# A stage boundary: the scan's first operands loaded from inside the projection stage

## The chip, the cores and the metric

The kernel runs on one core of a Trainium2 chip. The time is device microseconds (us) of one execution, and the figure for a kernel is the median of several runs.

## The reference, cut to what matters

The reference is a two-layer decoder trunk for 1024 tokens of width 1024, in float32: layer 0 is attention and a mixture of experts, layer 1 is a Mamba-2 mixer and a mixture of experts. The change lies in the Mamba-2 mixer:

```python
z, xbc, dt = jnp.split(h @ w_in, [D_INNER, D_INNER + XBC_DIM], axis=-1)
xbc = jax.nn.silu(causal_depthwise_conv(xbc, conv_w, conv_b))
xs, bm, cm = jnp.split(xbc, [D_INNER, D_INNER + SSD_GROUPS * D_STATE], axis=-1)
dt = jax.nn.softplus(dt + dt_bias)
a = -jnp.exp(a_log)
y = ssd_chunked_scan(xs, dt, a, bm, cm) + d_skip[:, None] * xs
y = y.reshape(Bsz, S, D_INNER) * jax.nn.silu(z)
y = rmsnorm(y.reshape(Bsz, S, SSD_GROUPS, -1), gate_norm.reshape(SSD_GROUPS, -1))
return y.reshape(Bsz, S, D_INNER) @ w_out
```

Per chunk of the scan, with `cs` the running sum of `dt * a`: `y = (C B^T * exp(cs_i - cs_j)) (dt x) + (C state) * exp(cs)`, and the state is decayed and receives `B^T (to_end * dt x)`.

## The kernel before, in words

The layer is three stages, each in a `Stage` of its own. A stage ends with its block: every engine is done, its semaphores are cleared, and all engines meet at a barrier before the next stage's first instruction.

**Projection** (`ssd_project_stage`). TensorE works off 80 units of 24 matmuls: 48 channel units (24 tiles of 128 channels, two halves of the tokens each) and 32 gate units (4 groups of 8 token tiles). In the last group the 8 gate units come last. ScalarE evicts each unit (`evict`): a channel unit into `u`, a gate unit through SiLU into one of two buffers `z`. A channel tile is then convolved on VectorE into `acc`, and `silu` on ScalarE writes `c`. SP stores `z` to the array Z (L1202) and `c` to XC (L1206) in DRAM; the eviction of gate unit m waits until the store of gate unit m-2 has landed, since there are two `z` buffers. TensorE writes a ring of four banks, so a unit waits for the eviction of the unit four before. The running sums are stored to CSR early in the stage. Weights come through three buffers `raw`.

**Scan** (`scan_stage`). 32 items, 8 chunks of 128 tokens for each of 4 groups of 8 heads. An item is spread over four engines. ScalarE: `falls` (L1686, eight activations, one for each head, that subtract sums from sums), a copy `bt` (L1695), one exponential over all heads (L1701), and the sum of squares of an earlier item; VectorE: five or six operations, of which `W` (L1735) needs the exponential; TensorE: `front` (L1625 to L1633) and `back` (L1642 to L1657); GpSimd: the fading of the state and the gate with `z` (L1789). Inputs are loaded for four items at a time into two sets of buffers: `bT`, `cT` (256 KB each), `xT` (1 MB), and `sums` (2 MB, rows of CSR spread over all partitions). The first `sums` go in four pieces of 512 KB, whose rows are 128 numbers long, not 512. SP issues the loads in this order:

```python
operands(0)
for n in range(RING):
    gates(n)
operands(1)
early_dma(sp)
for n in range(RING, NI):
    if n % LOAD == 0 and n >= 2 * LOAD:
        operands(n // LOAD)
    gates(n)
```

`operands(q)` loads the inputs of items 4q to 4q+3, `gates(n)` the gate values `z` of item n (L1599, four buffers; from item 4 on it waits for the gate of item n-4), and `early_dma` issues half of the output weights (`w_out`, 4 MB). The sums of set q = 2 and later are issued by ScalarE (L1700) in item 4q-5.

**Output** (`ssd_out_stage`): normalization, transposes and the product with `w_out`. Then comes the mixture of experts.

Of the kernel before, what the change touches and what calls it, by code (L numbers as in the profile page):

```python
# [23 lines left out]
P = 128  # L24
D = 1024
S = 1024
NT = S // P
ND = D // P
HALF = 512
# [14 lines left out]
DI, HS, G, N, HD = 2048, 32, 4, 128, 64  # L44
HG = HS // G
XBC = DI + 2 * G * N
SSD_IN = DI + XBC + HS
CONV = 4
# [1022 lines left out]
def ssd_project_stage(nc, K, A):  # L1071
# [4 lines left out]
    LEFT, GW, CPG = CONV - 1, DI // G, DI // G // P  # L1076
    TILES = [n for g in range(G) for n in (DI // P + g, DI // P + G + g, *range(CPG * g, CPG * (g + 1)))]
    PER = CPG + 2
    NTILES, RAW, PAR, BANKS, RING = len(TILES), 3, range(2), 4, 3
    UNITS = []  # L1080
    for g in range(G):
        tiles, gates = [(False, i, h) for i in range(PER * g, PER * (g + 1)) for h in range(2)], [(True, g, t) for t in range(NT)]
        UNITS += tiles + gates if g else gates + tiles
    NU = len(UNITS)
# [3 lines left out]
    PIECES = [('gate', 0, q) for q in range(QZ)] + [('tile', 0, 0), ('dt', 0, 0), ('tile', 1, 0)]  # L1088
# [12 lines left out]
    PIECES, WHEN = [PIECES[n] for n in order], [WHEN[n] for n in order]  # L1101
    number = {p: n for n, p in enumerate(PIECES)}
    splits = {u: [n for n in range(len(PIECES)) if WHEN[n] == u] for u in range(-1, NU)}
    with Stage(nc, "sproj") as st:
        raw = [st.sb(f"raw{j}", [P, D]) for j in range(RAW)]
        with ExitStack() as early:
            hn = [early.enter_context(nc.sbuf_tensor(f"sproj_hn{a}", [P, D], F32))[:, :] for a in PAR]

# [2 lines left out]
        gh, gl = ([st.sb(f"{n}{q}", [P, 2, GW], F32R) for q in range(QZ)] for n in ("gate_high", "gate_low"))  # L1111
        dh, dl = (st.sb(n, [P, ND, HS], F32R) for n in ("dt_high", "dt_low"))
        tap = st.sb("tap", [P, NTILES, CONV + 1])
        u, acc, c = ([st.sb(f"{n}{a}", [P, w]) for a in PAR] for n, w in (("u", LEFT + S), ("acc", S), ("c", S)))
        z = [st.sb(f"z{a}", [P, GW]) for a in PAR]

        pos = st.sb("pos", [P, NT, HS])
# [15 lines left out]
        c_stored, z_stored = ([st.sem(f"{n}_stored{a}") for a in PAR] for n in "cz")  # L1133
# [40 lines left out]
        @block.sync  # L1174
        def _(sp):
            def load(n):
                if n >= RAW:
                    sp.wait_ge(w_low, n - RAW + 1)
                sp.dma_start(raw_of(n), piece(n)[0]).then_inc(raw_loaded[n % RAW], 16)

            for t in range(NT):
                for k in PAR:
                    if t >= RING:
                        sp.wait_ge(added[k], t - RING + 1)
                    r = k * S + t * P
                    sp.dma_start(rows[k][t % RING], K.Y[r:r + P, :]).then_inc(got[k][t % RING], 16)
                load(t)
            sp.dma_start(tap[:, :, :], A["conv"].rearrange("k p n -> p k n")).then_inc(tap_loaded, 16)
            load(NT)
            for v in range(0, NU + 2):  # L1190
                for n in splits.get(v, ()):
                    if n + RAW < len(PIECES):
                        load(n + RAW)
                if v == NT + 11:
                    sp.wait_ge(sums_kept, 2)
                    for h in range(2):
                        sp.dma_start(K.CSR[:, half(h)], z[h][0:HS, :]).then_inc(sums_stored, 16)
                if v >= 1 and v <= NU and UNITS[v - 1][0]:
                    _, g, t = UNITS[v - 1]
                    m = gates_before(v - 1)  # L1200
                    sp.wait_ge(evicted, v)
                    sp.dma_start(K.Z[tile(t), g * GW:(g + 1) * GW], z[m % 2][:, :]).then_inc(z_stored[m % 2], 16)  # L1202
                if v >= 2 and not UNITS[v - 2][0] and UNITS[v - 2][2] == 1:
                    i = UNITS[v - 2][1]
                    sp.wait_ge(c_ok, i + 1)
                    sp.dma_start(K.XC[TILES[i], :, :], c[i % 2][:, :]).then_inc(c_stored[i % 2], 16)  # L1206
            for a in PAR:
                sp.wait_ge(z_stored[a], 16 * (G * NT // 2))
                sp.wait_ge(c_stored[a], 16 * (NTILES // 2))
            sp.nop()  # L1210

        @block.tensor
# [293 lines left out]
def scan_stage(nc, K, A, early_dma):  # L1506


    GW, KT = HG * HD, HG * HD // P
    ITEMS = [(g, c) for g in range(G) for c in range(NT)]  # L1510
    NI, RING, LOAD = len(ITEMS), 4, 4
    with Stage(nc, "scan") as st:
        PAR = range(2)
        xT = [st.sb(f"xT{a}", [P, KT, LOAD * P]) for a in PAR]
        bT, cT = ([st.sb(f"{n}{a}", [P, LOAD * P]) for a in PAR] for n in ("bT", "cT"))
        z, y = ([st.sb(f"{n}{a}", [P, GW]) for a in range(RING)] for n in "zy")
        sums = [st.sb(f"sums{a}", [P, HG, LOAD * P]) for a in PAR]
        cbm = [st.sb(f"cbm{a}", [P, P]) for a in PAR]
        dec, W = ([st.sb(f"{n}{a}", [P, HG, P]) for a in PAR] for n in ("dec", "W"))
        bt = [st.sb(f"bt{a}", [P, N]) for a in PAR]  # L1520
# [3 lines left out]
        pcb, pbt, pyi, pst = (st.ps(n, [P, HALF]) for n in ("pcb", "pbt", "pyi", "pst"))  # L1524
        px, py = ([st.ps(f"{n}{a}", [P, GW]) for a in PAR] for n in ("px", "py"))
        z_loaded, y_stored = ([st.sem(f"{n}{a}") for a in range(RING)] for n in ("z_loaded", "y_stored"))
        loaded, sums_loaded = ([st.sem(f"{n}{a}") for a in PAR] for n in ("loaded", "sums_loaded"))
        first_sums = [st.sem(f"first_sums{j}") for j in range(LOAD)]
        cb_done, x_turned, yi_done, st_done, y_done = (st.sem(n) for n in ("cb_done", "x_turned", "yi_done", "st_done", "y_done"))
        bt_ok, e_ok, ss_ok = (st.sem(n) for n in ("bt_ready", "decay_ready", "squares"))  # L1530
        cbm_ok, seg_ok, xdt_ok, yi_ok, y_ok, st_ok = (st.sem(n) for n in ("cbm_ready", "seg_ready", "xdt_ready", "yi_ready", "y_ready", "state_ready"))
# [28 lines left out]

        def sums_here(eng, n):

            if n < LOAD:
                eng.wait_ge(first_sums[n], 16)
            else:
                q = n // LOAD
                eng.wait_ge(sums_loaded[q % 2], (q // 2 + q % 2) * 16)

        def arrived(eng, n):
            eng.wait_ge(loaded[n // LOAD % 2], (n // (2 * LOAD) + 1) * 48)  # L1570
# [1 line left out]
        @block.sync  # L1572
        def _(sp):
            def inputs(g, tok, a):
                for buf, first in ((bT, DI // P), (cT, DI // P + G)):
                    sp.dma_start(buf[a][:, :], K.XC[g + first, :, tok]).then_inc(loaded[a], 16)
                sp.dma_start(xT[a][:, :, :], K.XC[g * KT:(g + 1) * KT, :, tok].rearrange("k p n -> p k n")).then_inc(loaded[a], 16)

            def operands(q):
                (g, c), a = ITEMS[q * LOAD], q % 2  # L1580
                tok = slice(c * P, (c + LOAD) * P)
                if q >= 2:
                    sp.wait_ge(y_done, (q - 1) * LOAD)
                if q == 0:
                    for j in range(LOAD):
                        sp.dma_start(sums[0][:, :, j * P:(j + 1) * P],
                                     K.CSR[0:HG, j * P:(j + 1) * P].partition_broadcast(P)).then_inc(first_sums[j], 16)
                        if j == 0:
                            inputs(g, tok, a)
                    return  # L1590
                inputs(g, tok, a)
                if q == 1:
                    sp.dma_start(sums[a][:, :, :], spread_sums(q)).then_inc(sums_loaded[a], 16)

            def gates(n):
                (g, c), a = ITEMS[n], n % RING
                if n >= RING:
                    sp.wait_ge(gated, n - RING + 1)
                sp.dma_start(z[a][:, :], K.Z[c * P:(c + 1) * P, g * GW:(g + 1) * GW]).then_inc(z_loaded[a], 16)  # L1599

            operands(0)
            for n in range(RING):
                gates(n)
            operands(1)
            early_dma(sp)
            for n in range(RING, NI):
                if n % LOAD == 0 and n >= 2 * LOAD:
                    operands(n // LOAD)
                gates(n)

            for t in range(2):
                for g in range(G // 2):
                    m = g * NT + t
                    sp.wait_ge(y_stored[m % RING], (m // RING + 1) * 16)
                sp.dma_start(K.y_first[t][:, :, :].rearrange("p g n -> p (g n)"),
                             K.YS[t * P:(t + 1) * P, 0:DI // 2]).then_inc(K.y_loaded[t], 16)
# [186 lines left out]
def ssd_out_stage(nc, K, A):  # L1803
# [5 lines left out]
    with Stage(nc, "sout") as st:  # L1809
        w, loaded = K.w_out, K.wo_loaded  # L1810
        wh, wl = (st.sb(n, [P, NK, D], F32R) for n in ("w_high", "w_low"))
        y, y_loaded, EARLY = K.y_first, K.y_loaded, 3
        whole = [st.sb(f"whole{a}", [P, NK, P]) for a in range(2)]
        yh, yl = ([st.sb(f"{n}{a}", [P, NK, P], F32R) for a in range(2)] for n in ("y_high", "y_low"))
        tp = [st.ps(f"tp{a}", [P, NK, P]) for a in range(2)]
        py = [st.ps(f"py{a}", [P, D]) for a in range(2)]
# [132 lines left out]
def ssd_layer(nc, K, A):  # L1949
    with Stage(nc, "ssd_layer") as outer:  # L1950
        ctx, K.wo_loaded = outer.ctx, outer.sem("wo_loaded")

        def sb(name, shape):
            return ctx.enter_context(nc.sbuf_tensor(name, shape, F32))

        K.heads, K.ss = sb("heads", [P, 7, NT, HS]), sb("gate_ss", [P, NT, G])
        with ExitStack() as early:
            K.HH, K.HL = (early.enter_context(nc.sbuf_tensor(f"ssd_{n}", [P, ND, S], F32R)) for n in ("high", "low"))
            ssd_project_stage(nc, K, A)
        K.w_out = sb("w_out", [P, DI // P // 2, D])  # L1960

        K.y_first = [sb(f"y_first{a}", [P, G // 2, DI // G]) for a in range(2)]
        K.y_loaded = [outer.sem(f"y_loaded{a}") for a in range(2)]

        def out_weights(sp):
            sp.dma_start(K.w_out[:, :, :], A["w_out_ssd"][0:DI // 2, :].rearrange("(k p) n -> p k n", p=P)).then_inc(K.wo_loaded, 16)

        scan_stage(nc, K, A, out_weights)
        ssd_out_stage(nc, K, A)
# [877 lines left out]
```

## Time and profile before

| | |
|---|---|
| median of 3 runs | 2892.21 us (2891.63 to 2892.35) |
| profiled execution, its own time | 2890.16 us |
| its span | 2888.4 us |
| TensorE / VectorE / ScalarE / GpSimd busy | 92% / 65% / 56% / 19% of the span |
| mean granted TensorE clock | 0.959 |

The profile is one execution. Its own time is 1.8 us more than its span, and 2.05 us below the median of the runs. Times in the rows are microseconds from the span's start; busy shares are averages over very different stages, and the change touches only the stretch from about 1760 to 1980 us: projection until 1782, scan until about 1983.

### The profile page before, as it was taken

The numbers are of one execution on the slowest core, as the hardware profiler recorded it, in microseconds if no ns is written. First come the engines' busy times: TensorE is split into PE (matmuls) and PEld (weight loads), VectorE is DVE, ScalarE is ACT, GpSimd is POOL, SyncE is SP. The second block draws the span as 40 slices with busy tenths as digits, with TensorE's granted clock in tenths as the row PEclk, the third lists the DMA queues.
The fourth block names the chain that finished last, engine by engine and source line by source line (L and its number), as shares of the span: only waits on it lengthen the run. The fifth ranks groups of instructions, "written<-read, shape, count | busy, mean of one in ns | idle before, by whom it ended". The sixth has DMA issues, their size and how long they took to land. (4 is left out here: it accounts for less than half of the span.)

```text
span 2888.4 us, 40193 instructions
## 1 busy us (share of the span) xinstructions
PE 2652.6 (92%) x13762; PEld 2134.6 (74%) x13762; DVE 1883.1 (65%) x2208; ACT 1604.7 (56%) x2027; POOL 542.9 (19%) x462
## 2 busy tenths in 40 slices
PE   8997999987999999967999997898998799999992
PEld 6885677765888888846788885686885688888881
DVE  6335766426888888854572450686454788888895
ACT  4134554324888888854331231784122688888882
POOL 0000000001444444420000000342000344444440
PEclk9998999998999999988999998998999899999996
DMA  4315110125999999963232322984114799999994
GB/s 159 87 46 167 38 45 23 37 106 193 372 380 382 384 388 383 377 248 99 72 119 78 109 84 89 328 282 140 46 35 155 262 391 386 373 380 379 381 373 191
DMA packets 240965, 618.68 MB, mean 214 GB/s; under 512 B 31864, under 2 KB 80528, under 8 KB 240720
## 3 DMA queue, kind: packets, MB, share of 16 engines
q1 hardware_dynamic: 209712, 558.35, 53.6%
q0 software_dynamic: 19136, 33.61, 3.1%
q10 hardware_dynamic: 12000, 25.17, 2.4%
q8 instruction: 73, 1.20, 0.2%
q14 instruction: 44, 0.36, 0.0%
HBM read 566.55 MB, written 86.13 MB: 226 GB/s over the span
## 5 line engine op out<-in xcount | busy, mean ns | idle before, releaser
L2527 DVE TENSOR_TENSOR moe_w_low<-moes_raw,moe_w_high 128x2048 fp32r<-128x2048 f32 x384 | 865.0, 2286 | 147.7 <-ACT moe_w_high L2456 147.5
L2456 ACT ACTIVATE moe_w_high<-moes_raw 128x2048 fp32r<-128x2048 f32 x384 | 721.6, 1914 | 68.9 <-PEq L150 54.6
L2321 POOL COPY moe_pick<-moes_tokens 128x1 int32 (+1 forms) x64 | 108.4, 1694 | 582.9 <-PE moe_px L2370 582.0
L174 PE MATMUL moe_py<-moe_w_high,moe_h_high 128*128 128x512 f32 x512 | 209.2, 409 | 0.0
L174 PE MATMUL moe_pg<-moe_w_high,moe_x_high 128*128 128x512 f32 x512 | 205.6, 402 | 3.8 <-DVE moe_x_low L2577 3.8
L174 PE MATMUL moe_pu<-moe_w_high,moe_x_high 128*128 128x512 f32 x512 | 204.2, 399 | 0.0
L176 PE MATMUL moe_pg<-moe_w_high,moe_x_low 128*128 128x512 f32 x512 | 201.7, 394 | 0.0
L175 PE MATMUL moe_pg<-moe_w_low,moe_x_high 128*128 128x512 f32 x512 | 201.0, 393 | 0.0
L176 PE MATMUL moe_py<-moe_w_high,moe_h_low 128*128 128x512 f32 x512 | 200.8, 392 | 0.0
L176 PE MATMUL moe_pu<-moe_w_high,moe_x_low 128*128 128x512 f32 x512 | 200.5, 392 | 0.0
L175 PE MATMUL moe_py<-moe_w_low,moe_h_high 128*128 128x512 f32 x512 | 200.0, 391 | 0.0
L175 PE MATMUL moe_pu<-moe_w_low,moe_x_high 128*128 128x512 f32 x512 | 199.6, 390 | 0.0
L923 ACT ACTIVATE att_pr<-att_pr,att_nmx 128x256 f32<-128x256 f32 (+7 forms) x128 | 99.2, 775 | 114.1 <-DVE att_nmx L880 113.2
L2033 POOL MEMSET moes_xg<- 128x1024 f32 x4 | 3.7, 962 | 837.8 <-POOLq L157 837.8
L174 PE MATMUL sproj_pm<-ssd_high,sproj_w_high 128*128 128x512 f32 x384 | 149.9, 390 | 0.0
L176 PE MATMUL sproj_pm<-ssd_high,sproj_w_low 128*128 128x512 f32 x384 | 149.4, 389 | 0.0
L175 PE MATMUL sproj_pm<-ssd_low,sproj_w_high 128*128 128x512 f32 x384 | 149.4, 389 | 0.0
L1305 ACT ACTIVATE sproj_u<-sproj_pm 128x512 f32<-128x512 f32 x48 | 28.8, 599 | 165.0 <-PE sproj_pm L176 165.0
L2334 POOL DMA_INDIRECT Y<-moe_y,moe_back x64 | 115.5, 1805 | 22.4 <-issue 22.4
L174 PEld LDWEIGHTS moe_pg<-moe_w_high,moe_x_high 128*128 128x128 f32 x512 | 97.1, 190 | 23.7 <-issue 4.4
L176 PEld LDWEIGHTS moe_pg<-moe_w_high,moe_x_low 128*128 128x128 f32 x512 | 97.0, 189 | 22.6
L880 DVE CUSTOM_DVE_ANT_0 att_pr<-att_sc,consts 128x256 f32<-128x256 f32 (+7 forms) x128 | 96.1, 751 | 25.9 <-PE att_sc L814 21.4
(398 smaller groups left out, 6117.5 us busy)
## 6 DMA issues: line engine op xcount, KB each, us to landing
moes_raw<-in_w_gate SPq DMA_DIRECT2D x128, 1024.0 KB, 8.4
moes_raw<-in_w_up SPq DMA_DIRECT2D x128, 1024.0 KB
moes_raw<-in_w_down SPq DMA_DIRECT2D x128, 1024.0 KB, 8.8
sproj_raw<-in_w_in_ssd SPq DMA_DIRECT2D x40, 512.0 KB
XC<-sproj_c SPq DMA_DIRECT2D x24, 512.0 KB, 5.1
scan_sums<-CSR ACTq DMA_DIRECT2D x6, 2048.0 KB, 12.0
HN<-plan_hn SPq DMA_DIRECT2D x16, 512.0 KB, 3.0
Z<-sproj_z SPq DMA_DIRECT2D x32, 256.0 KB, 2.4
```

The lines of the kernel that those rows point to most:

```text
L174: nc.tensor.matmul(out, lh, rh, start=start, stop=False)
L175: nc.tensor.matmul(out, lh, rl, start=False, stop=False)
L176: return nc.tensor.matmul(out, ll, rh, start=False, stop=stop)
L880: nc.vector.tensor_tensor_reduce(pr[n % RING][:, 0:w], sc[a][:, 0:w], m[:, S - w:S], 1.0, -NEG, ALU.add, ALU.min, nmx[:, n % RING:n % RING ...
L923: nc.scalar.activation(pr[r][:, 0:w], pr[r][:, 0:w], ACT.Exp, bias=nmx[:, r:r + 1], scale=-1.0, accum_out=den[:, r:r + 1]).then_inc(exped, 1)
L1305: nc.scalar.activation(u[i % 2][:, LEFT + h * HALF:LEFT + (h + 1) * HALF], pm[v % BANKS][:, :], ACT.Copy).then_inc(evicted, 1)
L2033: nc.gpsimd.memset(M.xg[a][:, :], 0.0).then_inc(cleared, 1)
L2321: nc.gpsimd.tensor_copy(pick[a][:, :], M.tokens[:, bass.ds(b, 1)]).then_inc(picked[a], 1)
L2334: nc.gpsimd.indirect_dma_start(out=Y[:, :], out_offset=bass.IndirectOffsetOnAxis(ap=back[a][:, :], axis=0), in_=y[a][:, :], in_offset=None ...
L2456: nc.scalar.activation(wh[c % SPLIT_SLOTS][:, :], M.raw[j][:, :], ACT.Copy).then_inc(w_high, 1)
L2527: nc.vector.tensor_tensor(wl[j][:, :], M.raw[c % RAW_SLOTS][:, :], bits(wh[j][:, :]), ALU.subtract).then_inc(w_low, 1)
```

## The change

The buffers `acc`, `c`, `u` of the projection and its third weight buffer `raw` move into one tile of the layer, `K.pre`. The first set of the scan's operand buffers is laid over the same memory. Four units before the end of the projection SP, after it has waited for everything that used this memory or writes what is loaded, issues the scan's first operands there, the sums as one 2 MB load. In the scan, SP no longer issues `operands(0)`; `operands(1)` comes after two gate loads rather than four, and the 4 MB of output weights go after the loads of item 8. Two buffers of the output stage are laid over `K.pre` too.

```diff
@@ ssd_project_stage
-        raw = [st.sb(f"raw{j}", [P, D]) for j in range(RAW)]
+        raw = [st.sb(f"raw{j}", [P, D]) for j in range(RAW - 1)] + [K.pre[:, 4 * S + 2 * (LEFT + S):5 * S + 2 * (LEFT + S)]]
-        u, acc, c = ([st.sb(f"{n}{a}", [P, w]) for a in PAR] for n, w in (("u", LEFT + S), ("acc", S), ("c", S)))
+        acc, c, u = ([K.pre[:, first + a * w:first + (a + 1) * w] for a in PAR] for first, w in ((0, S), (2 * S, S), (4 * S, LEFT + S)))
...
+                if v == NU - 4:
+
+                    sp.wait_ge(sums_stored, 32)
+                    sp.wait_ge(w_low, len(PIECES))
+                    for a in PAR:
+                        sp.wait_ge(c_stored[a], 16 * (NTILES // 2))
+                    K.first_operands(sp)
             for a in PAR:
                 sp.wait_ge(z_stored[a], 16 * (G * NT // 2))
-                sp.wait_ge(c_stored[a], 16 * (NTILES // 2))
@@ scan_stage
-        xT = [st.sb(f"xT{a}", [P, KT, LOAD * P]) for a in PAR]
-        bT, cT = ([st.sb(f"{n}{a}", [P, LOAD * P]) for a in PAR] for n in ("bT", "cT"))
+        xT = [K.xT, st.sb("xT1", [P, KT, LOAD * P])]
+        bT, cT = [K.bT, st.sb("bT1", [P, LOAD * P])], [K.cT, st.sb("cT1", [P, LOAD * P])]
...
-        sums = [st.sb(f"sums{a}", [P, HG, LOAD * P]) for a in PAR]
+        sums = [K.sums, st.sb("sums1", [P, HG, LOAD * P])]
...
-            if n < LOAD:
-                eng.wait_ge(first_sums[n], 16)
-            else:
-                q = n // LOAD
-                eng.wait_ge(sums_loaded[q % 2], (q // 2 + q % 2) * 16)
+            q = n // LOAD
+            eng.wait_ge(sums_loaded[q % 2], (q // 2 + 1) * 16)
...
-                if q == 0:
-                    for j in range(LOAD):
-                        sp.dma_start(sums[0][:, :, j * P:(j + 1) * P],
-                                     K.CSR[0:HG, j * P:(j + 1) * P].partition_broadcast(P)).then_inc(first_sums[j], 16)
-                        if j == 0:
-                            inputs(g, tok, a)
-                    return
...
-            operands(0)
-            for n in range(RING):
-                gates(n)
+            gates(0)
+            gates(1)
             operands(1)
-            early_dma(sp)
-            for n in range(RING, NI):
+            for n in range(2, NI):
                 if n % LOAD == 0 and n >= 2 * LOAD:
                     operands(n // LOAD)
                 gates(n)
+                if n == 2 * LOAD:
+                    early_dma(sp)
@@ ssd_out_stage
-        whole = [st.sb(f"whole{a}", [P, NK, P]) for a in range(2)]
+        whole = [K.pre[:, a * D:(a + 1) * D].rearrange("p (k n) -> p k n", n=P) for a in range(2)]
@@ ssd_layer
+        K.pre = sb("pre", [P, W + X + 2 * (HALF + CONV - 1)])
...
+        def first_operands(sp):
+
+            sp.dma_start(K.bT, K.XC[DI // P, :, 0:HALF]).then_inc(K.first_loaded, 16)
+            sp.dma_start(K.cT, K.XC[DI // P + G, :, 0:HALF]).then_inc(K.first_loaded, 16)
+            sp.dma_start(K.xT, K.XC[0:HG * HD // P, :, 0:HALF].rearrange("k p n -> p k n")).then_inc(K.first_loaded, 16)
+            sp.dma_start(K.sums, K.CSR[0:HG, 0:HALF].partition_broadcast(P)).then_inc(K.first_sums, 16)
```

## Rows read from the trace of the kernel before

**Rows 1.** Waits, 1780 to 1985: total us, times, longest

```profile
ACT scan_dec L1686 <- DMA scan_sums<-CSR: 28.5, 3, 13.9
PE scan_pcb L1625 <- DMA scan_xT<-XC: 20.2, 2, 19.1
DVE scan_W L1735 <- ACT scan_dec L1701: 9.8, 2, 8.4
```

**Rows 2.** Timeline, stage boundary: start, length, engine, what, idle before

```profile
1781.44 0.60 ACT L1301 ACTIVATE sproj_z<-sproj_pm 128x512 f32<-128x512 f32 x1 [4.84 <-PE sproj_pm L176]
...
1785.67 1.03 POOL L1780 TENSOR_TENSOR scan_skip<-consts,heads 128x512 f32<-128x512 f32 x1 [512.28 <-POOLq L157]
...
1795.66 2.44 ACT L1686 ACTIVATE scan_dec<-scan_sums,heads 128x128 f32<-128x128 f32 x8 [13.63 <-DMA scan_sums<-CSR]
...
1802.38 0.28 ACT L1695 ACTIVATE scan_bt<-scan_pbt 128x128 f32<-128x128 f32 x1 [4.27 <-PE scan_pbt L1633]
```

**Rows 3.** Timeline of VectorE, the operation W of items 0, 3, 4, 5, 31

```profile
1805.06 1.23 DVE L1735 TENSOR_TENSOR scan_W<-scan_dec,scan_cbm 128x1024 f32<-128x1024 f32 x1 [1.39 <-ACT scan_dec L1701]
...
1820.27 1.22 DVE L1735 TENSOR_TENSOR scan_W<-scan_dec,scan_cbm 128x1024 f32<-128x1024 f32 x1
...
1835.18 1.23 DVE L1735 TENSOR_TENSOR scan_W<-scan_dec,scan_cbm 128x1024 f32<-128x1024 f32 x1 [8.38 <-ACT scan_dec L1701]
...
1842.64 1.22 DVE L1735 TENSOR_TENSOR scan_W<-scan_dec,scan_cbm 128x1024 f32<-128x1024 f32 x1
...
1975.17 1.22 DVE L1735 TENSOR_TENSOR scan_W<-scan_dec,scan_cbm 128x1024 f32<-128x1024 f32 x1
```

**Rows 4.** Timeline of ScalarE at item 4

```profile
1815.57 0.38 ACTq L1700 DMA_DIRECT2D scan_sums<-CSR  x1
...
1830.99 0.40 ACT L1686 ACTIVATE scan_dec<-scan_sums,heads 128x128 f32<-128x128 f32 x1 [13.86 <-DMA scan_sums<-CSR]
```

**Rows 5.** Timeline of SP's queue: start and length of each DMA issue

```profile
1745.03 0.32 SPq L1206 DMA_DIRECT2D XC<-sproj_c  x1
...
1782.06 0.32 SPq L1202 DMA_DIRECT2D Z<-sproj_z  x1
...
1787.14 2.84 SPq L1577 DMA_DIRECT2D scan_xT<-XC  x1
1790.02 12.04 SPq L1586 DMA_DIRECT2D scan_sums<-CSR  x3
...
1812.38 0.76 SPq L1593 DMA_DIRECT2D scan_sums<-CSR  x1
1813.18 2.78 SPq L1966 DMA_DIRECT2D w_out<-in_w_out_ssd  x1
...
1860.58 0.43 SPq L1576 DMA_DIRECT2D scan_bT<-XC  x1
```

**Rows 6.** DMA issues by line: count, KB each, median us to landing

```profile
Z<-sproj_z SPq DMA_DIRECT2D x32, 256.0 KB, 2.4
...
scan_sums<-CSR SPq DMA_DIRECT2D x1, 2048.0 KB, 18.6
```

**Rows 7.** Line L1700, sums loads issued by ScalarE

```profile
DMA to landing us min/median/max: 11.3/12.0/18.4
```

**Rows 8.** Windows: us, busy and instructions by engine, PEclk, DMA share, GB/s

```profile
1776.00:1781.00 5.00, 5.00 (x23) 4.13 (x22) 0.00 (x0) 0.60 (x1) 0.00 (x0) 1.00 0.14 52
...
1790.00:1795.00 5.00, 0.00 (x0) 0.00 (x0) 0.00 (x0) 0.00 (x0) 0.00 (x0) 0.50 0.82 80
1795.00:1801.00 6.00, 0.52 (x2) 0.52 (x3) 0.00 (x0) 2.44 (x8) 0.00 (x0) 0.50 0.91 314
1801.00:1806.00 5.00, 4.72 (x16) 2.91 (x14) 2.52 (x4) 3.59 (x7) 0.00 (x0) 0.56 0.62 173
1806.00:1811.00 5.00, 4.57 (x34) 4.12 (x35) 3.95 (x7) 5.00 (x17) 0.00 (x0) 1.00 0.49 89
...
1831.00:1836.00 5.00, 1.65 (x6) 1.46 (x7) 0.82 (x1) 5.00 (x16) 0.00 (x0) 0.50 1.03 410
```

More of the change, by code:

```diff
@@ L1526, in scan_stage @@
         z_loaded, y_stored = ([st.sem(f"{n}{a}") for a in range(RING)] for n in ("z_loaded", "y_stored"))
-        loaded, sums_loaded = ([st.sem(f"{n}{a}") for a in PAR] for n in ("loaded", "sums_loaded"))
-        first_sums = [st.sem(f"first_sums{j}") for j in range(LOAD)]
+        loaded, sums_loaded = ([x, st.sem(f"{n}1")] for n, x in (("loaded", K.first_loaded), ("sums_loaded", K.first_sums)))
         cb_done, x_turned, yi_done, st_done, y_done = (st.sem(n) for n in ("cb_done", "x_turned", "yi_done", "st_done", "y_done"))
@@ L1956, in ssd_layer @@
         K.heads, K.ss = sb("heads", [P, 7, NT, HS]), sb("gate_ss", [P, NT, G])
+        W = HG * HALF
+        X = HG * HD // P * HALF
+        K.pre = sb("pre", [P, W + X + 2 * (HALF + CONV - 1)])
+        K.sums = K.pre[:, 0:W].rearrange("p (h n) -> p h n", n=HALF)
+        K.xT = K.pre[:, W:W + X].rearrange("p (k n) -> p k n", n=HALF)
+        K.bT, K.cT = (K.pre[:, W + X + n * HALF:W + X + (n + 1) * HALF] for n in range(2))
+        K.first_loaded, K.first_sums = outer.sem("first_loaded"), outer.sem("first_sums")
+        def first_operands(sp):
[3 more added lines that the diff above has]
+            sp.dma_start(K.sums, K.CSR[0:HG, 0:HALF].partition_broadcast(P)).then_inc(K.first_sums, 16)
+        K.first_operands = first_operands
         with ExitStack() as early:
```

## The prediction

> **What bounds the kernel now.** TensorE is busy 92% of the span, but an average says nothing about a boundary between two stages, so I first read the waits of the scan's stretch [rows 1]. Two waits for transfers stand out. ScalarE waited 28.5 us in all for `sums`, TensorE 20.2 us for `xT`. The timelines put them in two places.
>
> The first is the boundary. The last gate unit is evicted at 1781.44, and the engines are let into the scan at 1785.67, where GpSimd, which waits for no transfer, starts at once; ScalarE's first instruction starts only at 1795.66 and TensorE's first at about 1800.5, 19.1 us after its last [rows 1, 2]. Between, the DMA engines carry the 512 KB pieces of the sums at 80 GB/s with a busy share of 0.82, whereas 314 GB/s go by in the next stretch [rows 8], and SP itself needs 12.04 us to issue three of those pieces [rows 5].
>
> The second is item 4, the first that uses operand set 1. The clearest pulse of the scan is the operation W. Item 0 has it at 1805.06, item 3 at 1820.27, item 4 at 1835.18, item 5 at 1842.64, item 31 at 1975.17 [rows 3]. From item 5 on that is 132.53 / 26 = 5.10 us an item, a pace set by the engines (no transfer ends a wait there). Items 3 to 4 took 14.91 and 4 to 5 took 7.46: 9.81 + 2.36 = 12.17 us over the pace. The cause is in ScalarE's row: it waited 13.86 us until `sums` of set 1, issued by SP at 1812.38, had landed at 1830.99, 18.6 us later [rows 4 to 6]. That load was issued late because it stood behind the clogged first loads, and it shared the DMA engines with ScalarE's own 2 MB load issued at 1815.57 [rows 4].
>
> **The change part by part.** *The early loads.* Units are 4.84 + 0.60 = 5.44 us apart [rows 2], so unit 75 is evicted at 1781.44 - 4 x 5.44 = 1759.68, and SP reaches the new code at about 1760.6. Its waits are over by then: the last store of `c` was issued at 1745.03 [rows 5], and the sums and the last weights are older. It issues 256 + 256 + 1024 + 2048 KB = 3.67 MB. The queue is nearly empty (share 0.14 [rows 8]). At 314 GB/s this takes 11.7 us; with the 2.4 us that even a lone Z store needs to land [rows 6] it is in place at about 1775, before 1785.67. That the sums now come as 2 KB rows, not 512 B, is what lets me use 314 and not 80; both ends are kept below.
>
> *The start of the scan.* ScalarE starts at 1785.67, runs `falls` (2.44), then `bt`; from there to W it is 1805.06 - 1802.38 = 2.68 us [rows 2, 3]. TensorE's front of item 0 (from 1800.5 to 1802.38, under 2 us) and GpSimd's 1.03 us lie under `falls`. Item 0's W comes at 1785.67 + 2.44 + 2.68 = 1790.79, not 1805.06: 14.27 us gained. Were the first operands late, each microsecond past 1785.67 would be lost. Items 1 to 3 keep their 15.21 us, to 1806.0. An item's gate values are used only after its last matmuls, which wait for W, and their loads now go first.
>
> *Set 1.* SP issues two gate loads (0.32 each), `bT`, `cT` (0.43 each), `xT` (0.43 to 2.84, the clogged one) and the sums at 1787.6 to 1790.0 [rows 5]. Counted from 1785.7, 4.19 MB have to pass: 13.4 us at 314 GB/s plus 2.4, landing at 1801.5. ScalarE's `falls` of item 4 must start 1835.18 - 1830.99 = 4.19 us before W [rows 3, 4], and at the pace that W is at 1806.0 + 5.1 = 1811.1, so the deadline is 1806.9. The load is 5.4 us early, and the whole 12.17 us go. The upper bound is the longest landing seen, 18.6 us from 1790.0: 1.7 us past the deadline, and at worst also the 2.36 us of item 5, together 4.1 us. Neither of the two transfers that slowed it before is beside it from the start: `w_out` has moved back, and ScalarE's load is issued at about 1801.3.
>
> *The order of the other loads.* `w_out` (4.19 MB) is moved past `operands(2)` and the gate load of item 8, into a running scan. Behind it on SP's queue come gates 9 to 11 and `operands(3)`; beside it run ScalarE's sums of set 3. Those sums have 5 x 5.10 + 4.7 - 4.19 = 26.0 us from issue to need, and the longest such landing, beside `w_out`, was 18.4 [rows 7]. `operands(3)` is tighter. Its issue at 1860.58 is 17.9 us after W of item 5 and its use directly after W of item 11, 30.6 us after it, which leaves 12.7 us; `w_out` is issued about three items (15.3 us) before. In these 28.0 us 9.45 MB have to pass (w_out, three gates, 1.57 MB of operands, 2.10 MB of sums, three stores of results). At the 410 GB/s of a full queue with `w_out` in it [rows 8] this takes 23.0 + 2.4 = 25.4 us, at 314 it takes 32.5. I take no stall, since rows of 4 KB make up nearly half the bytes; the bounds are 0 and 4.5 us. The load of `w_out` itself is needed only after item 31, over 100 us later.
>
> *The rest.* The new addresses of buffers and the few semaphores less are costed at nothing: the same instructions run on the same shapes, and the projection's final wait for `c` was long fulfilled. After item 31 everything moves up rigidly behind a barrier.
>
> *Sum.* 14.27 + 12.17 = 26.4 us. The profiled execution's own time 2890.16 becomes 2863.8; it lies 2.05 us under the median of the runs, so the median becomes **2865.8 us**.
>
> **A rule against the change.** The projection's Z stores now queue behind 3.67 MB. The one of unit 76 is issued at about 1765.7, and units 78 and 79 may not be evicted before the stores of 76 and 77 have landed. By the sizes above these land at about 1777 and 1778; the eviction of 78 is due at 1776.0 and may slip by a microsecond, which costs nothing, since no later unit needs its bank; that of 79 is due at 1781.44. A lone Z store takes 2.4 us [rows 6], and if the stores could overtake the loads nothing would slip at all. The Trainium skill ("DMA: Bandwidth & Descriptors", section "Queues, rings and completion order") says that each DMA engine consumes the descriptors of one issuing engine's ring in order; by it the stores wait. The landing of 18.4 us of a ScalarE load beside a full SP queue, against 12.0 as the median [rows 7], fits engines that are shared, but says nothing of order inside one queue. The sum stays the same by either reading.
>
> **The rivals.**
> - *Set 1 still late.* The sums land past 1806.9. For it: 18.6 us was measured [rows 6]. Against it: nothing of that size runs beside it now. Costs 1.7 to 4.1 us: 2867.5 to 2869.9.
> - *`w_out` in the running scan* makes `operands(3)` late, up to 4.5 us: 2866 to 2870.3. For it: the average of the whole stretch leaves only 2.6 us of slack even at 410 GB/s.
> - *Z stores trapped.* If the early loads land 18.6 us after an issue drawn out to 1765, the store of 77 lands at about 1784.5 and the last eviction slips by 3 us: 2869.
> - *A slow TensorE clock.* The clock fell to the lower of its levels (granted 0.50, 1.2 GHz) while TensorE idled, and was back at 1.00 only at 1806, 5.5 us after its first matmul [rows 8]. Now item 0's `back` starts at about 1792, 6.5 us after the first matmul, but with more gaps between. If it still runs at the low level, its some 2.7 us double: 2868. The Trainium skill ("TensorE: Matmul & The Clock Gate", section "What's actually happening") says the slow state is the default and activity releases it; the trace agrees in both directions.
> - *The other side: the early loads crawl.* One mechanism: the spread of the sums runs at the 80 GB/s seen at the boundary [rows 8]. Then 3.67 MB take 46 us, the last Z stores wait behind them, and the last eviction comes at about 1810, 28.5 us late: 2892.21 - 26.4 + 28.5 = 2894.3. It decides when the loads take over 43 us, that is at under 85 GB/s; for a loss of over 0.2% they need under 75. Against it: rows of 2 KB, not 512 B, and 314 GB/s directly after.
> - *The change does not do what it says*: the early loads wait for something and go out after the last unit. Every wait is fulfilled by 1755 or so; I see nothing for it. At 314 GB/s they would land 11.7 + 2.4 us after 1785.7, near 1800, which takes back the whole first gain, and leave the second: some 2880.
>
> **How the numbers follow.** Forecast as summed, within 1.5 us: 0.48. Set 1 late 0.14, `w_out` 0.18, Z stores 0.06, clock 0.07, early loads useless 0.03, crawling loads 0.03, anything else 0.01. The likeliest gives 2865.8. Below it there is little room (no wait is left to remove), so the low end is 2862.5; the high end takes in each of the delays and two of them partly together: 2872. That leaves out about 0.12. A measurement of this kernel tells about 0.2%, 5.8 us, from no change; all cases but the crawling one are faster by more: faster 0.96, same 0.02, slower 0.02.
>
> **What would show it.** In the profile after: ScalarE's first `falls` and TensorE's first matmul within 1 us of GpSimd's first instruction, about 4 us after the last eviction; W of item 0 about 5.1 us later; no wait for `sums` over 2 us in the scan; W of items 3, 4 and 5 at 5.1 to 5.2 us; W of item 31 at 1948.8. Wrong would be: the last eviction later than 1781.4, a wait for `xT` at item 12, a TensorE clock under 1.00 from item 0's `back` on, or a later stage that takes longer than before.

## The result and the profile after

| | median of 4 runs (us) | all runs |
|---|---|---|
| before | 2891.92 | 2890.87 to 2892.35 |
| changed | 2874.99 | 2872.96 to 2875.13 |

The ratio is 0.9942, 95% interval 0.993 to 0.9954: 16.9 us faster, where 26.4 had been forecast. The time lies 3 us above the high end of the range. The profiled execution of the changed kernel took 2875.02 us.

First the operation W again, in the timeline of VectorE; of the changed kernel these are items 0, 3, 4, 5, then 11 and 12 (before: [rows 3]).

```profile
1792.22 1.23 DVE L1730 TENSOR_TENSOR scan_W<-scan_dec,scan_cbm 128x1024 f32<-128x1024 f32 x1 [1.83 <-ACT scan_dec L1696]
...
1807.43 1.22 DVE L1730 TENSOR_TENSOR scan_W<-scan_dec,scan_cbm 128x1024 f32<-128x1024 f32 x1
1812.59 1.22 DVE L1730 TENSOR_TENSOR scan_W<-scan_dec,scan_cbm 128x1024 f32<-128x1024 f32 x1
1817.76 1.22 DVE L1730 TENSOR_TENSOR scan_W<-scan_dec,scan_cbm 128x1024 f32<-128x1024 f32 x1
...
1848.16 1.22 DVE L1730 TENSOR_TENSOR scan_W<-scan_dec,scan_cbm 128x1024 f32<-128x1024 f32 x1
1862.40 1.22 DVE L1730 TENSOR_TENSOR scan_W<-scan_dec,scan_cbm 128x1024 f32<-128x1024 f32 x1
```

Items 3, 4 and 5 now follow each other at 5.16 us: the stall at set 1 is gone. But from item 11 to item 12 it takes 14.24 us, 9.14 over the pace of 5.10. No other step is long. Two places of the timeline show where things stand (before: [rows 2]). At the boundary ScalarE starts its first `falls` 4.1 us after it began the last eviction, together with GpSimd. The last row below is TensorE at item 12, after its wait.

```profile
1783.09 0.60 ACT L1307 ACTIVATE sproj_z<-sproj_pm 128x512 f32<-128x512 f32 x1 [3.85 <-PE sproj_pm L176]
1787.21 2.45 ACT L1681 ACTIVATE scan_dec<-pre,heads 128x128 f32<-128x128 f32 x8 [3.53 <-PEq L157]
...
1854.95 0.80 PE L1620 MATMUL scan_pcb<-scan_cT,scan_bT 128*128 128x128 f32 x2 [7.43 <-DMA scan_xT<-XC]
```

`xT` of set 3 was issued by SP at 1836.65, where SP's queue stood like this:

```profile
1816.38 1.20 SPq L1578 DMA_DIRECT2D pre<-XC  x2
1817.62 0.48 SPq L1579 DMA_DIRECT2D pre<-XC  x1
1821.18 0.32 SPq L1594 DMA_DIRECT2D scan_z<-Z  x1
1821.54 0.43 SPq L1977 DMA_DIRECT2D w_out<-in_w_out_ssd  x1
1826.35 9.30 SPq L1594 DMA_DIRECT2D scan_z<-Z  x3
1835.69 0.44 SPq L1578 DMA_DIRECT2D scan_bT<-XC  x1
1836.18 0.43 SPq L1578 DMA_DIRECT2D scan_cT<-XC  x1
1836.65 0.43 SPq L1579 DMA_DIRECT2D scan_xT<-XC  x1
```

The same view of the window 1821 to 1856 by queue (q1 is SP's, q10 ScalarE's) and by issue:

```profile
DMA packets 5960, 13.75 MB, mean 393 GB/s; under 512 B 280, under 2 KB 280, under 8 KB 5958
...
q1 hardware_dynamic: 3227, 8.34, 63.0%
q10 hardware_dynamic: 2731, 5.38, 40.3%
...
scan_sums<-CSR ACTq DMA_DIRECT2D x1, 2048.0 KB, 20.9
pre<-CSR ACTq DMA_DIRECT2D x1, 2048.0 KB
scan_z<-Z SPq DMA_DIRECT2D x6, 256.0 KB, 11.0
YS<-scan_y ACTq DMA_DIRECT2D x6, 256.0 KB, 12.7
scan_xT<-XC SPq DMA_DIRECT2D x1, 1024.0 KB, 18.3
```

The DMA engines were full for 35 us, at 393 GB/s, and `xT` took 18.3 us to land. My sum had 9.45 MB in 28 us; 13.75 MB went by in the 35. From the issue of the weights (1821.5) to the need (1847.5) there were only 26 us, in which 10.34 MB went by at 398 GB/s. So the rate of the sum was about right; its time and its bytes were not. Missing in it were: set 2, issued at 1816.4 to 1817.6, of whose 1.57 MB about half was still on its way when the weights went out (SP's queue moved 0.97 MB from 1816.4 to 1821.5); the sums of set 4 (2.1 MB), issued by ScalarE at 1843.2, 4.3 us before set 3 was needed; and result stores, six in these 35 us where I had counted three. Of the six gate loads in the view the sum had the three between the weights and set 3. How much of the delay each missing part cost, no run here separates.

The two profiled executions lie 15.1 us apart. The parts: 1.65 us lost before the first eviction of this stretch is looked at (the last eviction is at 1783.09, not 1781.44; the projection's first instruction was already 1.6 us late), 0.09 gained at the barrier, 14.40 gained between the scan's release and its first W (19.39 us before, 4.99 now), 2.97 gained from W of item 0 to W of item 31 (170.11 before, 167.14 now), and the remaining 0.7 lost after it. The 2.97 are 12.0 gained at items 4 and 5 and 9.1 given back at item 12. In the medians, 26.4 - 9.1 = 17.3 stands against 16.9 measured.

### The profile page after: what moved, and what is told of

Same layout as the page of the kernel before. It is cut to its first block and busy times, and to the rows that moved or that the text cites. A ratio compares the mean times of both kernels' runs of the same rounds, so it can differ in the third digit from the quotient of the medians.

```text
span 2873.2 us, 40191 instructions
## 1 busy us (share of the span) xinstructions
PE 2654.9 (92%) x13762; PEld 2137.5 (74%) x13762; DVE 1883.6 (66%) x2208; ACT 1605.4 (56%) x2027; POOL 544.7 (19%) x462
## 5 line engine op out<-in xcount | busy, mean ns | idle before, releaser
L1311 ACT ACTIVATE pre<-sproj_pm 128x512 f32<-128x512 f32 x48 | 28.8, 600 | 165.0 <-PE sproj_pm L176 165.0
L176 PEld LDWEIGHTS moe_pu<-moe_w_high,moe_x_low 128*128 128x128 f32 x512 | 96.1, 188 | 22.3
```

What stands on the lines that cost most here:

```text
L176: return nc.tensor.matmul(out, ll, rh, start=False, stop=stop)
L1311: nc.scalar.activation(u[i % 2][:, LEFT + h * HALF:LEFT + (h + 1) * HALF], pm[v % BANKS][:, :], ACT.Copy).then_inc(evicted, 1)
```

## The experiments

The theory after the result: (A) the 4 MB of output weights in the running scan made set 3 late. Its rival: (B) set 3 is late of itself at the new pace.

**The weights behind item 28**, where no operand load follows:

```diff
-                if n == 2 * LOAD:
+                if n == NI - LOAD:
                     early_dma(sp)
```

> The changed kernel with one move: the 4 MB of output weights are issued after the gate load of item 28, behind the last operand loads, not of item 8. Theory A (the weights, standing in SP's queue ahead of operand set 3, made xT of items 12 to 15 late): the step from W of item 11 to W of item 12 falls from 14.2 us to 5.1 or 5.2, no wait for xT is left, and the time falls by 9.1 us, to about 2866. Theory B (set 3 is late for another reason, since two sums loads and the stores already fill the DMA engines at the new pace): the stall stays at item 12 or comes at another set, and the time stays within 2 us of 2875. If the weights now arrive too late for the output stage, its first step waits for them and part of the 9 us comes back there.

Measured: 2865.31 us, ratio 0.9911 (0.9896 to 0.9926). The stall at item 12 is gone and no load wait is left; the output stage does not wait for its weights. That is (A). The profiled execution, at 2868.74 the slowest of its four (the others took 2864.1 to 2866.2), has a new delay at the start, though: W of items 0, 1 and 2.

```profile
1792.35 1.23 DVE L1730 TENSOR_TENSOR scan_W<-scan_dec,scan_cbm 128x1024 f32<-128x1024 f32 x1 [1.83 <-ACT scan_dec L1696]
...
1799.71 1.22 DVE L1730 TENSOR_TENSOR scan_W<-scan_dec,scan_cbm 128x1024 f32<-128x1024 f32 x1
...
1805.73 1.22 DVE L1730 TENSOR_TENSOR scan_W<-scan_dec,scan_cbm 128x1024 f32<-128x1024 f32 x1
```

The steps are 7.36 and 6.02 us where the changed kernel had 4.88 and 5.16: 3.3 us lost. The windows (columns as in [rows 8]) tell the cause. First the changed kernel, then this one, 1793 to 1797:

```profile
1793.00:1795.00 2.00, 1.41 (x13) 1.44 (x13) 2.00 (x5) 2.00 (x8) 0.00 (x0) 0.99 1.02 393
1795.00:1797.00 2.00, 2.00 (x20) 2.00 (x19) 0.95 (x2) 2.00 (x7) 0.00 (x0) 1.00 1.05 403
```

```profile
1793.00:1795.00 2.00, 1.32 (x7) 1.31 (x7) 2.00 (x5) 2.00 (x8) 0.00 (x0) 0.50 0.96 356
1795.00:1797.00 2.00, 2.00 (x12) 2.00 (x11) 0.57 (x1) 2.00 (x6) 0.00 (x0) 0.50 1.05 409
```

Here the granted clock stays at 0.50 (1.2 GHz) for all of item 0's `back`, 12 matmuls in 2 us instead of 20. It is the clock rival of the prediction. Seven of the profiles are of kernels with the same work at this boundary, and only this one shows the loss, so it comes and goes between executions.

**The weights behind set 1**, ahead of the gate loads of items 2 and up:

```diff
             operands(1)
+            early_dma(sp)
             for n in range(2, NI):
...
-                if n == 2 * LOAD:
-                    early_dma(sp)
```

> The changed kernel with the output weights issued directly behind operand set 1, where they stood before the change, ahead of the gate loads of items 2 and up. Theory A (only bytes ahead of set 3 matter, and the first 15 us of the scan have idle DMA time): no stall at item 12, W of item 12 about 5.1 us after W of item 11, time about 2866, if gates 2 and 3, now behind 4 MB, still arrive for their items; these have about 15 us from issue, the weights take 10 to 14, so a wait of 0 to 4 us at the gate of item 2 is possible: 2866 to 2870. Theory B (move of the weights does not matter): 2875.

Measured: 2868.15 us, ratio 0.9917 (0.9904 to 0.9931). No stall at item 12, as (A) says. But the step to item 5 takes 10.81 us and the next 6.91, 7.5 us over the pace: GpSimd waited for the gate load of item 2.

```profile
1817.70 1.26 POOL L1783 TENSOR_TENSOR scan_y<-scan_yi,scan_z 128x512 f32<-128x512 f32 x1 [10.23 <-DMA scan_z<-Z]
```

I had expected at most 4 us there. In this execution the first 15 us of the scan did not have room for set 1, 4 MB and the gates. The five executions lie between 2861.74 and 2871.74, so the stall is perhaps not of this size in each of them; only one was profiled.

**The early loads alone**, the scan's other loads in the order before:

```diff
-            operands(0)
             for n in range(RING):
                 gates(n)
             operands(1)
             early_dma(sp)
             for n in range(RING, NI):
```

> The first part of the change alone: first operands loaded inside the projection, but the scan's other loads in the order before (four gate loads, operand set 1, output weights, then the rest). Theory A (the stall at item 12 comes from the weights' new place): none at item 12. Gates 2 and 3 are now ahead of the weights, so the wait for a gate load at item 2, seen when the weights went behind two gate loads, is gone too; gate 4 lands near its need, 0 to 3 us late. Time 2864 to 2868, some 8 us under the full change. Rival (the new order is what lets set 1 arrive in time): set 1 misses item 4 by 2 us or more and the time is 2868 to 2876.

Measured: 2871.57 us, ratio 0.9927 (0.9913 to 0.994). Set 1 is in time (ScalarE waited 0.7 us for its sums, and the step to item 4 is 5.17 us), so the new order of the gate loads is not what removes the stall at item 4. But the time is not that of the kernel with the weights at item 28, and my expectation missed a stall: now set 2 is late, at item 8 (a step of 13.03 us).

```profile
1833.10 0.79 PE L1619 MATMUL scan_pcb<-pre 128*128 128x128 f32 x2 [6.60 <-DMA pre<-XC]
```

The weights, issued at 1790.0, landed only after 29.5 us, at 1819.5, and set 2 was issued at 1815.4 to 1816.4. So the place of the weights is not one bad place: in one piece, and with ScalarE's 2 MB of sums beside them, they were still in the way of the set that came next. How the two queues shared the engines is seen best here, from 1805 to 1815 (weights on q1, sums and stores on q10):

```profile
q1 hardware_dynamic: 637, 2.61, 68.9%
q10 hardware_dynamic: 638, 1.27, 32.9%
```

The five executions took 2866.83 to 2873.39; the profiled one is the slowest.

**The layout alone** (all buffers where the change has them, all loads where and in the order they were):

> The kernel before with the new memory layout only: buffers of the projection, of operand set 0 and of the output stage in the shared tile, all loads where and in the order they were. Theory: addresses cost nothing, the time stays within 1.5 us of 2891. Rival: the layout itself slows or speeds a stage, more than 2 us either way, with a stage of the projection or the output stage longer in the trace.

Measured: 2892.02 us, ratio 0.9999 (0.999 to 1.0009). The addresses cost nothing, as the prediction had it.

**The weights at item 8 in the kernel before**:

```diff
             operands(1)
-            early_dma(sp)
             for n in range(RING, NI):
                 if n % LOAD == 0 and n >= 2 * LOAD:
                     operands(n // LOAD)
                 gates(n)
+                if n == 2 * LOAD:
+                    early_dma(sp)
```

> The kernel before with one part of the change alone: the output weights issued after the gate load of item 8; the first operands and the four gate loads as before. Theory A (what stands behind the sums of set 1 in SP's queue does not delay them): the stall at items 4 and 5 keeps 10 to 12 us, and a stall of 5 to 9 us appears at item 12; time 2891 + 5 to 9 = 2896 to 2900. Rival (the weights behind set 1 shared the engines with it and made it land only after 18.6 us): set 1 lands after 12 to 14 us, the stall at item 4 shrinks by some 5 us, and the time is 2891 to 2895.

Measured: 2900.21 us, ratio 1.0036 (1.0024 to 1.0048): slower by 8.6 us in the medians (runs from 2897.88 to 2906.06), and in the profile by one step, item 12, of 13.77 us. The step to item 4 is 14.98 us, as before (14.91), and the sums of set 1 took 18.9 us to land (before 18.6), although no weights stood behind them.

```profile
ACT scan_dec L1687 <- DMA scan_sums<-CSR: 29.5, 3, 14.5
```

So what was issued behind the sums on SP's queue did not delay them. In the kernel before, the weights were loaded at no cost, in the stall at item 4. And the price of their new place does not depend on the early loads: 8.6 us over the pace here, 9.1 with them.

**The weights issued by ScalarE** at item 7:

```diff
                 if n >= 2:
                     squares(n - 2)
+                if n == 7:
+                    early_dma(act)
```

> The changed kernel with the output weights issued at nearly the same time, item 7, but by ScalarE, so that on SP's queue nothing of them stands ahead of operand set 3; the bytes are the same. Theory A1 (order inside SP's queue made xT late): xT of set 3 lands within 12 us of its issue, no stall at item 12, time near 2866, perhaps 1 to 3 us more because stores of results now stand behind the weights on ScalarE's queue. Theory A2 (only the sum of bytes on the shared engines counts): xT still lands after some 18 us, the stall stays at 7 to 9 us and the time near 2875.

Measured: 2871.03 us, ratio 0.9929 (0.9914 to 0.9944). `xT` of set 3 landed after 15.7 us and the step to item 12 is 13.18 us. In the stall that is nearer to A2 than to A1: one microsecond less, not nine; the median lies between the two. Two things blur it. ScalarE issued the weights at 1825.6, 4.1 us later in the trace than SP had. And TensorE waited only 4.93 us for `xT`, not 7.43, but then ran at a granted clock of 0.50 until 1855 and 0.63 until 1858, which took most of that back. In the window 1836 to 1851:

```profile
DMA packets 2379, 6.12 MB, mean 408 GB/s; under 512 B 130, under 2 KB 130, under 8 KB 2378
...
q10 hardware_dynamic: 1274, 4.00, 66.8%
q1 hardware_dynamic: 1104, 2.12, 36.7%
```

Both queues have loads under way all this time and get similar numbers of packets, but q10, with the weights' rows of 4 KB, gets 4.00 MB and q1, with rows of 2 KB, 2.12 MB. The Trainium skill ("DMA: Bandwidth & Descriptors", section "Queues, rings and completion order") says that an engine takes turns between queues packet by packet; the traces agree, with 1274 packets against 1104 here and 637 against 638 with the early loads alone. The packets that the profile counts are of 2 to 4 KB here, about a row each; how many of them an engine takes from one queue before it turns to the other is not shown. Moving a load to another queue takes it out of the line, but the line then moves at half speed or less: q1 got 2.12 of 6.12 MB.

**Half of the weights at item 8, half behind item 28**:

```diff
-                if n == 2 * LOAD:
-                    early_dma(sp)
+                if n == 2 * LOAD:
+                    early_dma(sp, 0)
+                if n == NI - LOAD:
+                    early_dma(sp, 1)
```

> The changed kernel with half of the output weights (2 MB) behind item 8's gate load, the other half behind item 28's. Bytes theory: 2.1 MB less at about 400 GB/s land xT of set 3 5.2 us earlier, so the stall at item 12 shrinks from 9.1 us to 3.5 to 4; time 2869 to 2870. Rival (a fixed price of interrupting the queue): the stall stays over 7 us, time 2873 or more.

Measured: 2866.68 us, ratio 0.9921 (0.9904 to 0.9937), runs from 2863.21 to 2871.8. The step to item 12 is 5.64 us: 0.5 us of stall, not 3.5 to 4. `xT` landed after 10.9 us instead of 18.3. This profile is of the fastest of the four executions; the slowest took 8.6 us more, so the stall may have been longer there, which no trace shows. A fixed price of interrupting the queue (2873 us or more) is excluded by all four. In the profile the price is not in proportion to the bytes either, for two reasons that the traces show. Up to some 10.7 us of landing are free, since `xT` is issued that long before TensorE turns to it; here TensorE waited 0.26 us:

```profile
1845.69 0.49 PE L1622 MATMUL scan_pcb<-scan_cT,scan_bT 128*128 128x128 f32 x2 [0.26 <-DMA scan_xT<-XC]
```

And the 2.1 MB less took 7.4 us off the landing, not the 5.2 that I had expected at 400 GB/s. That is 284 GB/s, between the full rate and the half of it that is left beside ScalarE's sums of set 4; which of these bytes passed beside them I did not isolate. The rest of the 9.1 us, 9.14 - 7.43 = 1.7, is no waiting for bytes: the chain of engines had to fill again behind item 12, with TensorE at its low clock (granted 0.52 from 1855 to 1858 in the changed kernel).

**The weights in 8 loads of 512 KB**, behind the gate loads of items 8, 10, ... 22:

```diff
-                if n == 2 * LOAD:
-                    early_dma(sp)
+                if n >= 2 * LOAD and n % 2 == 0 and n < 2 * LOAD + 16:
+                    early_dma(sp, n // 2 - LOAD)
```

> The changed kernel with the output weights in 8 loads of 512 KB, one behind the gate load of items 8, 10, ... 22. Bytes-over-time theory: the scan at its pace moves 5.8 MB in 20.4 us, 283 GB/s of some 400; 512 KB each 10.2 us add 51 GB/s, so no set comes late, no stall over 0.5 us, time as with the weights at item 28, 2864 to 2867. Rival (any load put between the operand sets delays them noticeably, whatever its size): stalls of 1 us or more at several sets, 2868 or more.

Measured: 2864.74 us, ratio 0.991 (0.9893 to 0.9926), runs from 2863.26 to 2867.32. No step over 5.2 us; `xT` of set 3 landed after 7.9 us. The same 4 MB in the running scan cost nothing when spread.

**The first operands two units before the end** (and the weights behind item 28):

```diff
-                if v == NU - 4:
+                if v == NU - 2:
```

> The weights behind item 28's gate load, and the first operands issued two units before the end of the projection, not four, at about 1772 instead of 1762. Theory D (stores wait in SP's queue behind the loads): the first operands land at about 1785 to 1787, the Z store of unit 78, issued near 1777, lands with them after 8 to 10 us, the one of unit 79 after 3 to 5 us, so the stage ends 1 to 4 us later than with four units; time 2866 to 2870. Rival (stores pass the loads, only first operands' own landing counts): the Z stores land after 2.4 to 3 us, the scan starts on time but waits for its operands 0 to 1 us; time 2865 to 2866.

Measured: 2866.83 us, ratio 0.9919 (0.9903 to 0.9936). The Z store issued behind the loads landed after 10.1 us, at 1786.4, just after the last of the loads, at 1785.8. The medians alone (1.5 us over the kernel with the weights at item 28) are no proof, but the boundary is: from the last eviction to the scan's first instruction ScalarE idled 6.50 us, against 3.53.

```profile
1781.14 0.60 ACT L1307 ACTIVATE sproj_z<-sproj_pm 128x512 f32<-128x512 f32 x1 [4.84 <-PE sproj_pm L176]
1788.24 2.45 ACT L1681 ACTIVATE scan_dec<-pre,heads 128x128 f32<-128x128 f32 x8 [6.50 <-PEq L157]
```

The stores did wait in SP's queue behind the loads, and four units are early enough to hide it.

**TensorE fed across the boundary** (and the weights behind item 28): 12 matmuls more after the last unit, their result not used.

```diff
+            pe.wait_ge(evicted, NU - 3)
+            for k in range(4):
+                split_product(nc, pm[(NU - 4) % BANKS][:, :], (K.HH[:, k, tile(NT - 1)], K.HL[:, k, tile(NT - 1)]),
+                              (gh[k // 2][:, k % 2, :], gl[k // 2][:, k % 2, :]), k == 0, k == 3)
```

> The weights behind item 28's gate load, and besides 12 more matmuls on TensorE after the last gate unit, whose result nobody reads: they fill 2.7 of the some 4.2 us in which TensorE idles at the boundary while the last Z store lands. Theory C (the time of this kernel differs from run to run by some 3 us because item 0 of the scan meets the low TensorE clock in some runs): granted clock stays 1.00 across the boundary, the step from W of item 0 to W of item 1 is 4.9 us, and the median falls from 2865.3 by 0 to 3 us with less spread. Rival: the clock falls anyway during the sparse work of items 0 and 1, nothing changes; or the 12 matmuls hold up the stage's end, and it gets 1 to 3 us slower.

Measured: 2863.5 us, ratio 0.9903 (0.9886 to 0.9919), the lowest median of this study; its runs lie within 2.0 us (2862.14 to 2864.16), those without the matmuls within 4.6. In its profile the clock nevertheless fell, later, during items 0 and 1, and was back for item 0's `back`:

```profile
1787.00:1789.00 2.00, 0.75 (x5) 0.56 (x5) 1.29 (x2) 1.98 (x8) 0.10 (x1) 0.85 0.74 220
1789.00:1791.00 2.00, 2.00 (x7) 1.17 (x5) 0.00 (x0) 1.99 (x3) 0.00 (x0) 0.50 0.83 236
```

So the expectation that it stays at 1.00 was wrong. Whether the matmuls helped is open: the intervals of the two versions overlap, and versions without them also had profiles with no loss at item 0.

One execution of each kernel was profiled. The table has the time from W of item 0 to W of item 31 and the steps over 5.3 us:

| kernel | us | long steps: item (us) |
|---|---|---|
| before | 170.11 | 4 (14.91), 5 (7.46) |
| layout only | 170.47 | 4 (15.05), 5 (7.68) |
| before, weights at item 8 | 178.51 | 4 (14.98), 5 (7.18), 12 (13.77) |
| changed | 167.14 | 12 (14.24) |
| early loads only | 166.27 | 8 (13.03) |
| weights by ScalarE | 166.08 | 12 (13.18) |
| weights behind set 1 | 165.45 | 5 (10.81), 6 (6.91) |
| weights behind item 28 | 161.41 | 1 (7.36), 2 (6.02) |
| half of the weights | 158.55 | 12 (5.64) |
| weights in pieces | 158.08 | none |
| two units before the end | 158.07 | none |
| fed | 158.07 | none |

The executions of one kernel differ most where 2 or 4 MB go out in one piece ahead of a load that is needed soon: by 10.0 us with the weights behind set 1, 8.6 with half of them, 8.2 in the kernel before with the weights at item 8, 6.6 with the early loads alone. It is not a rule, since the changed kernel's own lie within 2.2 us. One profile for each kernel does not tell which step varies.

## Why the prediction was wrong

- *Start of the scan: right.* 14.27 us were forecast; 14.40 came. W of item 0 follows the release of the engines by 4.99 us, where 5.12 had been added up.
- *Set 1 and items 4 and 5: right.* Of the 12.17 us 12.04 went. The sums of set 1 landed after 12.3 us, at 1801.8, where 1801.5 had been worked out; that these two figures meet is partly luck, since the scan began 1.5 us later than in the sum and the bytes then went by at 370 to 381 GB/s, not 314.
- *Order of the other loads: here it failed.* "I take no stall, since rows of 4 KB make up nearly half the bytes; the bounds are 0 and 4.5 us." The mechanism, the place and even the item were in the text as a rival, with a chance of 0.18; the size was 9.1 us, twice the upper bound. Three mistakes made it small. The need was put 12.7 us after the issue of the set, counted from `bT`, its first load; TensorE turned to the set 11.8 us after that, which is 10.9 after the issue of `xT` (1854.95 - 7.43 - 1836.65). The bytes were counted from the issue of the weights on, as if the queues were empty then; they held about half of set 2. And ScalarE's next load, the sums of set 4, was left out, but it was issued 4.3 us before the need, and `xT`, once late, shared the engines with it until it landed. The average that I had worked out, 2.6 us of slack at full rate with empty queues at the start, should have been read as no slack.
- *The Z stores behind the early loads: right.* One eviction, that of unit 78, slipped by 1.0 us (it waited for a store that landed after 11.2 us), and nothing followed from it.
- *The clock rival: right in its mechanism, and near in size* (2.2 to 2.7 us in the forecast, 3.3 measured in one execution), though not in the changed kernel's own profile.
- *The other side* did not happen: the early loads did not crawl, the Z store queued directly behind all 3.67 MB of them landed 16 us after the first was issued.
- *Addresses and layout at nothing: right* (0.9999).

Without the weights' new place the sum would have held: 2865.31 and 2864.74 were measured for the two versions that put them elsewhere, and 2865.8 had been forecast. The early loads are worth 26 us where the weights are out of the way; the weights' new place gives 9 of them back.

## What to carry to other kernels

When a stall is removed, look at what was being loaded in it: here 4 MB travelled free in the stall at item 4, and wherever they went in one piece afterwards, ahead of a load that the scan still needed, they made a new one of 7 to 9 us. A load that is needed late belongs behind the last urgent one, or in pieces small enough for the spare rate (512 KB each 10 us cost nothing, 2 MB at once 0.5 us in the execution that was profiled, 4 MB at once 9 us). And a sum of bytes against a deadline has to begin with what is already in the queues and end with what joins them before the late transfer lands.

## What was unexpected of the hardware

- Two busy queues got packets in nearly equal numbers (637 and 638, and 1274 and 1104), so the one with rows of 4 KB moved 2.1 and 1.9 times the bytes of the one with rows of 2 KB. A big load with long rows on the other queue slows a small one with short rows more than its share of requests suggests.
- The stall grew out of proportion with the load: 0.5 us for 2 MB, 9.1 us for 4 MB at the same place, one execution each. The first 10.7 us of the landing are hidden and those behind are not, and a transfer that is late meets the next one.
- TensorE's clock, after 4 us of idling, stayed at 0.50 through item 0's `back` in one execution and was back at 1.00 within about a microsecond of its start in six others with the same boundary; that alone is 3.3 us.
- After 12 extra matmuls, with 1.46 us of idling left, the clock still fell to 0.50 a few microseconds later (granted 0.85 from 1787 to 1789, with TensorE busy 0.75 of these 2 us, and 0.50 until 1791).
